# One core, one encoder block: weights of two column tiles interleaved word by word, and moving buffers shifted by 64 bytes

## The chip, the cores and the metric

The kernel runs on one NeuronCore of a Trainium2 chip. The number that counts is device time in microseconds for one execution. "Span" is the time from the first to the last instruction in a profiled execution; the time of that same execution also takes in what lies around it.

Five engines work side by side: TensorE (PE in the rows; its weight loads are listed as PEld), VectorE (DVE), ScalarE (ACT), GpSimd (POOL) and SyncE (SP), which issues the DMAs. A matrix product on TensorE has two operands in SBUF: the stationary one (up to 128 columns, brought in by a weight load) and the moving one (here up to 512 columns, streamed through).

## The reference, cut to what matters

```python
h = _rmsnorm(x, norm_g)                      # 512 tokens x 2048
proj = h @ w_in                              # 2048 x 10304: A's q, k, v, gate; B's cq, ckv, kr, gate; merge gates
oa = _diff_attention(...)                    # 8 heads, two softmaxes per head, 512 x 512
ya = (norm(oa) * silu(ag)) @ w_oa            # 1024 x 2048
q, kv = norm(cq) @ w_uq, norm(ckv) @ w_ukv   # 512-wide latents, 8 heads
ob = _mla_attention(...)
yb = (ob * silu(bg)) @ w_ob
merged = sigmoid(ga) * ya + sigmoid(gb) * yb
out = _rmsnorm(x + merged @ w_out, final_g)
```

Everything is float32.

## The kernel before

**Three products for one.** Each float32 operand is kept as two float32r parts, `hi` (a rounded copy) and `lo` (what the rounding left). The helper `three` issues for each 128 x 128 stationary tile three matmuls into the same PSUM tile: hi with hi (line 2115 of the profile), stationary hi with moving lo (line 2116) and stationary lo with moving hi (line 2117). Every matmul is preceded by its own weight load, so the high stationary tile is loaded twice in a row and then the low one once. Nearly all of the kernel's matmuls come from `three` with 512 moving columns; the attention's value products (`pv`) have 256, transposes (lines 2168, 2460, 2598) have 128.

**Stages, in order of time.** First (about 0 to 480 us) the value columns and the merge gates: `h_hi`/`h_lo` are stationary, the weights `m_hi`/`m_lo` move; five groups of 1024 columns go through a Strassen scheme whose sums of blocks are the stationary `s12_hi`, `s12_lo`, `s34_hi`, `s34_lo`. Then the eight heads of branch A, the compressed latents of B, and the eight heads of B (about 480 to 1100 us). Here `project` takes a weight piece of 1024 words per partition (eight column tiles of 128) as the stationary operand and `h_hi`/`h_lo` move; `up` does the same with `c_hi`/`c_lo` moving; `rotary_keys` uses a full tile and a half tile of 64 columns. Between the tiles of a piece lie the matmuls of the attention of the previous head (`a_extras`, `b_extras`: scores, transposes, value products). In `token_values` and in the Y stage (about 1100 to 1240 us, the products with `w_oa` and `w_ob`) the same weight buffers are the moving operand instead. Last comes the product with `w_out`, again by the Strassen scheme.

**How a weight piece gets ready.** A DMA puts it into one of four slots of `w_raw`; ScalarE copies it to `w_hi` (`split_hi`, line 781); VectorE subtracts and writes `w_lo` over `w_raw` (`split_lo`, line 1385); TensorE waits on `lo_ready`. The splits run two pieces ahead of their use (`AHEAD`).

**Addresses.** Every SBUF tensor has a fixed place, given in KB from a base that is a multiple of 2 KB. Tiles start at multiples of 512 bytes within them. So every stationary and every moving operand of the 512-column matmuls starts at the same position of a 512-byte grid.

Of the kernel before, what the change touches and what calls it, by code (L numbers as in the profile page):

```python
# [24 lines left out]
P = 128  # L25
# [17 lines left out]
AHEAD = 2  # L43
# [28 lines left out]

HALF_T, HALF_K = SEQ // 2, KT // 2
M_GROUPS, GROUP = 5, 1024
OUT_G = M_GROUPS
# [153 lines left out]
def hybrid_encoder(nc, x, positions, norm_g, w_in, lam_q1, lam_k1, lam_q2, lam_k2, a_subln_g, w_oa,  # L229
                   q_norm_g, w_uq, kv_norm_g, w_ukv, w_ob, w_out, final_g, consts, out):  # L230
    ctx = ExitStack()
    with ctx:
        KB = 1024
        base = (nc.sbuf_base + 2 * KB - 1) // (2 * KB) * (2 * KB)

        def at(name, kb, shape, dt=F32):
            return nc.alloc_sbuf_tensor_at(name, shape, dt, offset=base + int(kb * KB))
# [8 lines left out]
        spare = at("spare", 0, [P, KT, SEQ])  # L246
        h_raw1 = at("h_raw1", 144, [P, KT, HALF_T])
# [11 lines left out]
        post_x = at("post_x", 156, [P, 2 * SEQ])  # L259
        m_hi = at("m_hi", 160, [P, M_HI, 4 * SEQ], F32R)  # L260
        s34_raw = at("s34_raw", 184, [P, HALF_K, 2, HALF_T])
        s34_lo = at("s34_lo", 184, [P, HALF_K, 2, HALF_T], F32R)
        post_z = at("post_z", 200, [P, 2 * SEQ])

# [6 lines left out]
        w_hi = at("w_hi", 112, [P, SLOTS, 1024], F32R)  # L271
        c_hi = at("c_hi", 128, [P, 2 * LT, SEQ], F32R)
        rope_n = at("rope_n", 128, [P, SEQ])
        c_lo = at("c_lo", 144, [P, 2 * LT, SEQ], F32R)
# [64 lines left out]
        v_raw = at("v_raw", 202, [P, TOK, P])  # L339
        ones_sq = at("ones_sq", 204, [P, P], F32R)  # L340
        cst = at("cst", 204.5, [P, P + 2])
        small = at("small", 205.03125, [P, 160])
# [3 lines left out]
        assert base + 206 * KB - 336 <= nc.sbuf_usable_end  # L346

# [430 lines left out]
        def _(act):  # L778
            def split_hi(piece, cols=2 * HALF_PIECE):
# [418 lines left out]
            for s in range(C_STEPS):  # L1198
                if s == VB_STEP:
                    a_step(s, Head(HEADS, C0), False, True)  # L1200
                split_hi(Piece(C0 + s + AHEAD), HALF_PIECE if s == C_STEPS - 1 else 2 * HALF_PIECE)
# [86 lines left out]
            for s in range(2):  # L1288
                split_hi(Piece(B0 + B_STEPS * last + s + AHEAD))
                b_step(s, last, LAST_PAIR, True, True)  # L1290
# [10 lines left out]
            for s in range(Y_STEPS):  # L1301
                if s >= Y_STEPS - AHEAD:
                    merge_hi(OUT0 + s + AHEAD - Y_STEPS)
                elif s not in (2, 3):
                    split_hi(Piece(Y0 + s + AHEAD))
                if s < 2:
# [5 lines left out]
                if s in (2, 3):  # L1312
                    split_hi(Piece(Y0 + s + AHEAD))
                if s == 2:
# [59 lines left out]
        def _(dve):  # L1374
# [6 lines left out]

            def split_lo(piece, cols=2 * HALF_PIECE):

                dve.wait_ge(hi_ready, piece.after(0))
                dve.tensor_tensor(w_lo[:, piece.slot, 0:cols], w_raw[:, piece.slot, 0:cols],  # L1385
                                  w_hi[:, piece.slot, 0:cols].bitcast(F32), ALU.subtract).then_inc(lo_ready, 1)

# [477 lines left out]
            def kr_split_lo(piece):  # L1865
                dve.wait_ge(hi_ready, piece.after(0))
                of_tiles = w_hi[:, piece.slot, :].rearrange("p (k c) -> p k c", k=8)[:, :, B_ROPE:2 * B_ROPE]
                raw_tiles = w_raw[:, piece.slot, :].rearrange("p (k c) -> p k c", k=8)[:, :, B_ROPE:2 * B_ROPE]
                dve.tensor_tensor(of_tiles, raw_tiles, of_tiles.bitcast(F32), ALU.subtract).then_inc(lo_ready, 1)

            for s in range(C_STEPS):
                if KR_STEP <= s + AHEAD < VB_STEP:
                    kr_split_lo(Piece(C0 + s + AHEAD))
                else:
                    if s == VB_STEP:
                        a_step(s, Head(HEADS, C0), False, True)
                    split_lo(Piece(C0 + s + AHEAD), HALF_PIECE if s == C_STEPS - 1 else 2 * HALF_PIECE)
                if s < VB_STEP:
# [83 lines left out]
            for s in range(2):  # L1962
                split_lo(Piece(B0 + B_STEPS * last + s + AHEAD))
                b_step(s, last, LAST_PAIR, True, True)
# [39 lines left out]
            for s in range(Y_STEPS):  # L2004
# [3 lines left out]
                if s == Y_STEPS - 1:  # L2008
                    merge_lo(OUT0)
                elif s < Y_STEPS - AHEAD and s not in (2, 3):  # L2010
                    split_lo(Piece(Y0 + s + AHEAD))
                if s < 2:
# [5 lines left out]
                if s in (2, 3):  # L2018
                    split_lo(Piece(Y0 + s + AHEAD))
                for head in GATED_AT.get(s, ()):  # L2020
# [91 lines left out]
        def _(pe):  # L2112
# [5 lines left out]

            def tile(piece, c0, width=P):
                return w_hi[:, piece.slot, c0:c0 + width], w_lo[:, piece.slot, c0:c0 + width]  # L2120

            def project(piece, dst, half, halves, rhs_hi, rhs_lo, k0, midway=None):

                pe.wait_ge(lo_ready, piece.after(0))
                for k in range(8):
                    if k == 4 and midway:
                        midway()
                    hi, lo = tile(piece, k * P)
# [334 lines left out]
            def rotary_keys(s):  # L2463
                piece = Piece(C0 + s)
                pe.wait_ge(lo_ready, piece.after(0))
                for k in range(8):
                    if k == 4:
                        tail(2 * s)
                    kt = 8 * (s % 2) + k
                    both = w_hi[:, piece.slot, k * P:(k + 1) * P]  # L2470
                    high = w_hi[:, piece.slot, k * P:k * P + B_ROPE]
                    if kt == 0:
# [13 lines left out]
            def token_values(g):  # L2486
                pieces = [Piece(C0 + VB_STEP + 2 * g + half) for half in range(2)]
                for t in range(TOK):
# [7 lines left out]
                    for kt in range(LT):  # L2496
                        if t == 0 and kt % 2 == 0:
                            pe.wait_ge(lo_ready, pieces[kt // 2].after(0))
                        hi, lo = tile(pieces[kt // 2], kt % 2 * SEQ, SEQ)
                        last = three(SC[2 + j % 2][:, :], c_hi[:, kt, q], c_lo[:, kt, q], hi, lo, kt == 0, kt == LT - 1)  # L2500
# [18 lines left out]

            def up(piece, c0, dst, which, stride=2 * P):  # L2520
                for k in range(LT):
                    hi, lo = tile(piece, k * stride + c0)
                    last = three(dst[:, :], hi, lo, c_hi[:, which * LT + k, :], c_lo[:, which * LT + k, :],
# [21 lines left out]
            def b_up(h, pair, prev):  # L2545
# [6 lines left out]
                if pair[1] == LOW:  # L2552
                    if prev:
                        pe.wait_ge(rope_cos, pair[0])
                    up(piece, P, TR, 1).then_inc(rope_up, 1)
                pe.wait_ge(acc_read, g - 1)
                up(piece, 0, b_banks(pair)[0], 1, 2 * P if pair[1] == LOW else P).then_inc(used, 1)
# [4 lines left out]
                up(piece, 0, b_banks(pair)[1], 0, P).then_inc(used, 1)  # L2562
                b_extras(1, h, pair, True, prev)
# [18 lines left out]
            def y_block(u, i, t, halves):  # L2582
# [3 lines left out]
                for k in range(2):  # L2586
                    hi, lo = tile(Piece(Y0 + U_STEPS * u + i), k * SEQ, SEQ)
                    kt = 2 * i + k
# [102 lines left out]
```

## Time and profile before

| | |
|---|---|
| median of 3 runs | 1430.33 us (1429.76 to 1430.56) |
| time of the profiled execution | 1429.3 us |
| span of the profiled execution | 1427.5 us |
| TensorE busy | 1413.2 us (99% of the span), 6604 matmuls |
| VectorE busy | 1020.0 us |
| ScalarE busy | 707.1 us |

The profiled execution took 1.8 us more than its span, and is 1.0 us below the median. "Busy" of TensorE is modelled from pipelined matmuls that overlap each other, so the time from the start of one matmul to the start of the next (called a gap below) tells more than the duration of one.

### The profile page before, as it was taken

What the parts mean: (1) busy time and instruction counts of PE and PEld (TensorE: products, weight loads), DVE (VectorE), ACT (ScalarE), POOL (GpSimd) and SP (SyncE); (2) the same over time, 40 slices, a digit from 0 to 9 for tenths busy, and PEclk for the clock granted to TensorE, in tenths of its full rate; (3) what the DMA queues carried; (4) which work ended last, traced back from release to release, by engine and by line L of the source; (5) the groups of instructions that cost most, each with busy time, mean ns of one, the idle gap of its engine ahead of it and who ended that gap; (6) DMA issues with size and microseconds to landing.
All of it is one profiled execution on the core that took longest, in us unless ns stands there. A gap on an engine that the chain in (4) does not pass through costs nothing.

```text
span 1427.5 us, 17881 instructions
## 1 busy us (share of the span) xinstructions
PE 1413.2 (99%) x6604; PEld 1175.1 (82%) x6604; DVE 1020.0 (71%) x1381; ACT 707.1 (50%) x894; POOL 31.5 (2%) x52
## 2 busy tenths in 40 slices
PE   8999999999999999999999999999999999999997
PEld 7888888888888888888888878888888888888886
DVE  6967898798878868677667656666676353478966
ACT  6546334544344456665666667555564222324434
POOL 0000000000000000000000000000000000000000
PEclk9999999999999999999999999999999999999999
DMA  8439576766756543222222434322242444617674
GB/s 300 145 125 316 177 263 186 236 213 212 238 184 207 184 146 83 79 82 81 81 81 82 114 106 133 84 72 66 81 140 74 151 125 152 207 45 247 197 254 172
DMA packets 182976, 218.43 MB, mean 153 GB/s; under 512 B 19456, under 2 KB 133248, under 8 KB 182272
## 3 DMA queue, kind: packets, MB, share of 16 engines
q1 hardware_dynamic: 174304, 197.64, 44.5%
q10 hardware_dynamic: 8608, 19.93, 3.6%
q8 instruction: 41, 0.67, 0.2%
q14 instruction: 23, 0.19, 0.0%
HBM read 195.51 MB, written 22.02 MB: 152 GB/s over the span
## 4 chain that ended last, share of the span: by engine, by line
PE 91%; DVE 3%; DMA 1%; ACT 1%; issue 1%; SPq 1%; POOL 0%; DVEq 0%; POOLq 0%; ACTq 0%
PE duo L2115 28%; PE duo L2117 28%; PE duo L2116 28%; PE duo L2168 2%; DMA start_y<-start_columns 1%; PE duo L2142 1%; PE duo L2145 1%; SPq L610 1%; ACT m_hi L886 1%; PE duo L2159 1%; PE duo L2164 1%; PE duo L2163 1%; PE duo L2160 1%; PE duo L2161 1%; PE duo L2598 0%
## 5 line engine op out<-in xcount | busy, mean ns | idle before, releaser
L1385 DVE TENSOR_TENSOR w_lo<-w_raw,w_hi 128x1024 fp32r<-128x1024 f32 (+1 forms) x116 | 135.3, 1167 | 99.3 <-ACT w_hi L781 98.7
L2115 PE MATMUL duo<-h_hi,w_hi 128*128 128x512 f32 x512 | 201.8, 394 | 0.0
L2117 PE MATMUL duo<-h_hi,w_lo 128*128 128x512 f32 x512 | 199.6, 390 | 0.0
L2116 PE MATMUL duo<-h_lo,w_hi 128*128 128x512 f32 x512 | 199.6, 390 | 0.0
L886 ACT ACTIVATE m_hi<-m_raw 128x2048 fp32r<-128x2048 f32 (+1 forms) x66 | 115.5, 1752 | 144.6 <-PE duo L2117 71.5
L781 ACT ACTIVATE w_hi<-w_raw 128x1024 fp32r<-128x1024 f32 (+1 forms) x118 | 119.2, 1011 | 124.3 <-DMA w_raw<-in_w_ob_dram 65.8
L1502 DVE TENSOR_TENSOR m_lo<-m_raw,m_hi 128x2048 fp32r<-128x2048 f32 (+3 forms) x71 | 141.9, 2001 | 26.9 <-ACT m_hi L886 26.5
L2115 PE MATMUL duo<-m_hi,h_hi 128*128 128x512 f32 x368 | 144.6, 393 | 1.6 <-DVE h_lo L1538 0.9
L2117 PE MATMUL duo<-m_hi,h_lo 128*128 128x512 f32 x368 | 143.3, 389 | 0.0
L2115 PE MATMUL duo<-m_hi,s_hi 128*128 128x512 f32 x320 | 124.5, 389 | 0.0
L2117 PE MATMUL duo<-m_hi,s_lo 128*128 128x512 f32 x320 | 124.5, 389 | 0.0
L2116 PE MATMUL duo<-m_lo,h_hi 128*128 128x512 f32 x300 | 116.8, 389 | 0.0
L2117 PEld LDWEIGHTS duo<-h_hi,w_lo 128*128 128x128 f32 x512 | 96.1, 188 | 20.6
L2116 PEld LDWEIGHTS duo<-h_lo,w_hi 128*128 128x128 f32 x512 | 96.3, 188 | 18.7
L2115 PEld LDWEIGHTS duo<-h_hi,w_hi 128*128 128x128 f32 x512 | 96.2, 188 | 18.7
L2116 PE MATMUL duo<-m_lo,s_hi 128*128 128x512 f32 x224 | 87.1, 389 | 0.0
L2115 PEld LDWEIGHTS duo<-m_hi,h_hi 128*128 128x128 f32 x368 | 69.1, 188 | 19.3 <-DVE m_lo L1502 2.4
L2117 PEld LDWEIGHTS duo<-m_hi,h_lo 128*128 128x128 f32 x368 | 69.1, 188 | 14.5
L1396 DVE TENSOR_TENSOR pt<-duo,pt 128x512 fp32r<-128x512 f32 x64 | 42.7, 687 | 45.7 <-ACT pt L794 45.5
L801 ACT ACTIVATE e<-e,small 128x512 f32<-128x512 f32 x64 | 45.8, 716 | 50.0 <-DVE small L1416 50.0
L2117 PEld LDWEIGHTS duo<-m_hi,s_lo 128*128 128x128 f32 x320 | 60.1, 188 | 12.5
L794 ACT ACTIVATE pt<-duo 128x512 fp32r<-128x512 f32 x64 | 36.3, 595 | 68.7 <-PE duo L2168 67.0
(322 smaller groups left out, 2991.0 us busy)
## 6 DMA issues: line engine op xcount, KB each, us to landing
m_raw<-in_w_in_dram SPq DMA_DIRECT2D x110, 512.0 KB, 4.7
w_raw<-in_w_in_dram SPq DMA_DIRECT2D x132, 256.0 KB, 3.0
o_raw<-in_w_out_dram SPq DMA_DIRECT2D x32, 512.0 KB, 5.1
spare<-in_w_in_dram SPq DMA_DIRECT2D x17, 512.0 KB, 4.6
h_raw<-in_w_in_dram SPq DMA_DIRECT2D x17, 512.0 KB, 4.9
w_raw<-in_w_oa_dram SPq DMA_DIRECT2D x32, 256.0 KB, 3.3
sig<-gates SPq DMA_DIRECT2D x8, 1024.0 KB, 6.3
w_raw<-in_w_ob_dram SPq DMA_DIRECT2D x32, 256.0 KB, 3.4
```

What stands on the lines that cost most here:

```text
L610: sp.dma_start(dst, src).then_inc(m_in[st.raw], 16)
L781: act.activation(w_hi[:, piece.slot, 0:cols], w_raw[:, piece.slot, 0:cols], ACT.Copy).then_inc(hi_ready, 1)
L794: act.activation(pt[:, 0, :, (t % 2) * P:(t % 2 + 1) * P], src[:, :].rearrange("p (k c) -> p k c", k=TOK), ACT.Copy).then_inc(pt_hi_ready, 1)
L801: last = act.activation(e[:, t % 2, m, :], e[:, t % 2, m, :], ACT.Exp, bias=nm[:, b:b + 1], scale=A_SCALE, accum_out=sums[:, b:b + 1])
L886: act.activation(hi_of(st, 0, st.parts), raw_of(st, 0, st.parts), ACT.Copy).then_inc(m_hi_ready, 1)
L1385: dve.tensor_tensor(w_lo[:, piece.slot, 0:cols], w_raw[:, piece.slot, 0:cols], w_hi[:, piece.slot, 0:cols].bitcast(F32), ALU.subtract).the ...
L1396: dve.tensor_tensor(pt[:, 1, :, c], src[:, :].rearrange("p (k c) -> p k c", k=TOK), pt[:, 0, :, c].bitcast(F32), ALU.subtract).then_inc(pt ...
L1502: dve.tensor_tensor(lo_of(st, p0, p1), raw_of(st, p0, p1), hi_of(st, p0, p1).bitcast(F32), ALU.subtract).then_inc(done, 1)
L2115: pe.matmul(dst, lhs_hi, rhs_hi, start=start, stop=False)
L2116: pe.matmul(dst, lhs_hi, rhs_lo, start=False, stop=False)
L2117: return pe.matmul(dst, lhs_lo, rhs_hi, start=False, stop=stop)
L2168: last = pe.transpose(dst[:, k * P:(k + 1) * P], src[:, k * P:(k + 1) * P], ident)
```

## The change

It has two parts.

First, the layout of `w_hi` when it is used as the stationary operand. Before, its column tiles lay one after the other. Now the first half and the second half of a piece alternate word by word: word 0 of tile 0, word 0 of tile 4, word 1 of tile 0, and so on. ScalarE's copy reads `w_raw` in order and writes with a step of two words; VectorE's subtraction reads `w_hi` with a step of two; the weight load of a high tile reads 128 words with a step of two (a tile covers 1024 bytes instead of 512). `w_lo` stays as it was, since it lies over `w_raw`. Pieces that are used as the moving operand (`moving=True`) keep the old layout. `kr_split_lo` follows the new layout with one more dimension.

Second, the places. The base becomes a multiple of 512 bytes. At 32, 144 and 184 KB 512 bytes are left free, and `h_hi`, `m_hi`, `c_hi`, `s34_lo` and some more (`spare`, `s34_raw`, `post_z`, `rope_n`, `ones_sq`, `cst`, `small`) start 64 bytes past the grid. `h_lo`, `m_lo`, `c_lo`, `w_hi`, `w_lo`, `s12_hi`, `s12_lo`, `s34_hi` and the operands of attention and of the last stages stay on it.

```diff
+BANKS, ROOM_AT, MOVED_BY = 512, (32, 144, 184), 64
+def in_halves(columns):
+    return columns.rearrange("p (j q) -> p j q", j=2)
+def in_pairs(columns):
+    return columns.rearrange("p (q j) -> p j q", j=2)
...
-        base = (nc.sbuf_base + 2 * KB - 1) // (2 * KB) * (2 * KB)
+        base = (nc.sbuf_base + BANKS - 1) // BANKS * BANKS
+        def at(name, kb, shape, dt=F32, off=0):
+            room = BANKS * sum(kb >= edge for edge in ROOM_AT)
+            return nc.alloc_sbuf_tensor_at(name, shape, dt, offset=base + int(kb * KB) + room + off)
...
-        h_hi = at("h_hi", 0, [P, KT, SEQ], F32R)
+        h_hi = at("h_hi", 0, [P, KT, SEQ], F32R, off=MOVED_BY)
-        m_hi = at("m_hi", 160, [P, M_HI, 4 * SEQ], F32R)
+        m_hi = at("m_hi", 160, [P, M_HI, 4 * SEQ], F32R, off=MOVED_BY)
-        s34_lo = at("s34_lo", 184, [P, HALF_K, 2, HALF_T], F32R)
+        s34_lo = at("s34_lo", 184, [P, HALF_K, 2, HALF_T], F32R, off=MOVED_BY)
-        c_hi = at("c_hi", 128, [P, 2 * LT, SEQ], F32R)
+        c_hi = at("c_hi", 128, [P, 2 * LT, SEQ], F32R, off=MOVED_BY)
...
-                act.activation(w_hi[:, piece.slot, 0:cols], w_raw[:, piece.slot, 0:cols], ACT.Copy
-                               ).then_inc(hi_ready, 1)
+                dst, src = w_hi[:, piece.slot, 0:cols], w_raw[:, piece.slot, 0:cols]
+                if not moving:
+                    dst, src = in_pairs(dst), in_halves(src)
+                act.activation(dst, src, ACT.Copy).then_inc(hi_ready, 1)
...
+                dst, src, hi = (a[:, piece.slot, 0:cols] for a in (w_lo, w_raw, w_hi))
+                if not moving:
+                    dst, src, hi = in_halves(dst), in_halves(src), in_pairs(hi)
+                dve.tensor_tensor(dst, src, hi.bitcast(F32), ALU.subtract).then_inc(lo_ready, 1)
...
-            def tile(piece, c0, width=P):
-                return w_hi[:, piece.slot, c0:c0 + width], w_lo[:, piece.slot, c0:c0 + width]
+            def high_tile(piece, k, tiles=8):
+                half = tiles // 2
+                c0 = k % half * P
+                return in_pairs(w_hi[:, piece.slot, 0:tiles * P])[:, k // half, c0:c0 + P]
+            def tile(piece, k, tiles=8):
+                return high_tile(piece, k, tiles), w_lo[:, piece.slot, k * P:(k + 1) * P]
```

## Rows read from the trace of the kernel before

**Rows 1.** The page: engines' busy time, and the slices of TensorE and its clock.

```profile
PE 1413.2 (99%) x6604; PEld 1175.1 (82%) x6604; DVE 1020.0 (71%) x1381; ACT 707.1 (50%) x894; POOL 31.5 (2%) x52
PE   8999999999999999999999999999999999999997
PEclk9999999999999999999999999999999999999999
```

**Rows 2.** The page: the chain that ended last, shares by engine.

```profile
PE 91%; DVE 3%; DMA 1%; ACT 1%; issue 1%; SPq 1%; POOL 0%; DVEq 0%; POOLq 0%; ACTq 0%
```

**Rows 3.** Waits of TensorE: us in total, times, longest (six rows in all).

```profile
PE duo L2216 <- DMA cst<-in_consts_dram: 2.6, 1, 2.6
...
PE duo L2115 <- DVE h_lo L1502: 0.3, 1, 0.3
```

**Rows 4.** Groups of TensorE's matmuls, shapes apart: busy us, mean ns of one (tiles: moving, stationary).

```profile
L2115 PE MATMUL duo<-h_hi,w_hi 128*128 128x512 f32 x512 | 201.8, 394 | 0.0
...
L2116 PE MATMUL duo<-h_lo,w_hi 128*128 128x512 f32 x512 | 199.6, 390 | 0.0
...
L2115 PE MATMUL duo<-m_hi,s_hi 128*128 128x512 f32 x320 | 124.5, 389 | 0.0
...
L2115 PE MATMUL duo<-c_hi,w_hi 128*128 128x512 f32 x80 | 32.5, 406 | 0.0
...
L2474 PE MATMUL duo<-h_lo,w_hi 128*64 128x512 f32 x16 | 6.4, 410 | 0.0
L2476 PE MATMUL duo<-h_hi,w_hi 128*128 128x512 f32 x15 | 5.9, 393 | 0.0
```

**Rows 5.** TensorE's timeline in the Y stage, first and last of 178 rows: start us, us.

```profile
1104.78 0.39 PE L2115 MATMUL duo<-w_hi,ga_hi 128*128 128x512 f32 x1
...
1144.90 0.39 PE L2115 MATMUL duo<-w_hi,gb_hl 128*128 128x512 f32 x1
```

**Rows 6.** TensorE's timeline in an A head: a value product and the projection behind it.

```profile
552.56 0.28 PE L2115 MATMUL duo<-pt,v_hl 128*128 128x256 f32 x1
552.67 0.28 PE L2116 MATMUL duo<-pt,v_hl 128*128 128x256 f32 x1
...
553.87 0.28 PE L2117 MATMUL duo<-pt,v_hl 128*128 128x256 f32 x1
553.99 0.40 PE L2115 MATMUL duo<-h_hi,w_hi 128*128 128x512 f32 x1
554.23 0.40 PE L2116 MATMUL duo<-h_lo,w_hi 128*128 128x512 f32 x1
554.46 0.39 PE L2117 MATMUL duo<-h_hi,w_lo 128*128 128x512 f32 x1
...
555.15 0.39 PE L2117 MATMUL duo<-h_hi,w_lo 128*128 128x512 f32 x1
```

**Rows 7.** The chain in order of time, one group of four transposes in an A head.

```profile
591.33 0.44 PE duo L2168 x4
```

**Rows 8.** Groups of weight loads, shapes apart: busy us, mean ns of one.

```profile
L2116 PEld LDWEIGHTS duo<-h_lo,w_hi 128*128 128x128 f32 x512 | 96.3, 188 | 18.7
...
L2474 PEld LDWEIGHTS duo<-h_lo,w_hi 128*64 128x64 f32 x16 | 2.1, 134 | 0.6
```

**Rows 9.** Timeline of the weight loads in an A head.

```profile
609.89 0.19 PEld L2116 LDWEIGHTS duo<-h_lo,w_hi 128*128 128x128 f32 x1
```

**Rows 10.** TensorE's timeline from the same moment, first and last of 12 rows.

```profile
609.89 0.39 PE L2115 MATMUL duo<-h_hi,w_hi 128*128 128x512 f32 x1
...
612.38 0.39 PE L2117 MATMUL duo<-h_hi,w_lo 128*128 128x512 f32 x1
```

**Rows 11.** Line 781, the copy to `w_hi`: duration ns min/median/max.

```profile
L781 ACT ACTIVATE w_hi<-w_raw x118: 615/1053/1067, 481.0 to 1237.6; 128x1024 fp32r<-128x1024 f32 x106, 128x512 fp32r<-128x512 f32 x12
```

**Rows 12.** Line 1385, the subtraction to `w_lo`, and who waited for it (no row follows).

```profile
L1385 DVE TENSOR_TENSOR w_lo<-w_raw,w_hi x116: 680/1224/1230, 484.6 to 1238.7; 128x1024 fp32r<-128x1024 f32 x104, 128x512 fp32r<-128x512 f32 x12
...
who waited for it (us, times):
```

**Rows 13.** Busy time by stretch: PE, PEld, DVE, ACT, POOL, clock, DMA share, GB/s.

```profile
600.00:650.00 50.00, 50.00 (x240) 41.62 (x239) 34.44 (x70) 32.21 (x52) 4.28 (x6) 1.00 0.28 80
```

More of the change, by code:

```diff
@@ L1200, in _ @@
                     a_step(s, Head(HEADS, C0), False, True)
-                split_hi(Piece(C0 + s + AHEAD), HALF_PIECE if s == C_STEPS - 1 else 2 * HALF_PIECE)
+                split_hi(Piece(C0 + s + AHEAD), HALF_PIECE if s == C_STEPS - 1 else 2 * HALF_PIECE,
+                         moving=VB_STEP <= s + AHEAD < C_STEPS)
                 if s < VB_STEP:
@@ L1288, in _ @@
             for s in range(2):
-                split_hi(Piece(B0 + B_STEPS * last + s + AHEAD))
+                split_hi(Piece(B0 + B_STEPS * last + s + AHEAD), moving=True)
                 b_step(s, last, LAST_PAIR, True, True)
@@ L1304, in _ @@
                 elif s not in (2, 3):
-                    split_hi(Piece(Y0 + s + AHEAD))
+                    split_hi(Piece(Y0 + s + AHEAD), moving=True)
                 if s < 2:
@@ L1312, in _ @@
                 if s in (2, 3):
-                    split_hi(Piece(Y0 + s + AHEAD))
+                    split_hi(Piece(Y0 + s + AHEAD), moving=True)
                 if s == 2:
@@ L1876, in _ @@
                         a_step(s, Head(HEADS, C0), False, True)
-                    split_lo(Piece(C0 + s + AHEAD), HALF_PIECE if s == C_STEPS - 1 else 2 * HALF_PIECE)
+                    split_lo(Piece(C0 + s + AHEAD), HALF_PIECE if s == C_STEPS - 1 else 2 * HALF_PIECE,
+                             moving=VB_STEP <= s + AHEAD < C_STEPS)
                 if s < VB_STEP:
@@ L1962, in _ @@
             for s in range(2):
-                split_lo(Piece(B0 + B_STEPS * last + s + AHEAD))
+                split_lo(Piece(B0 + B_STEPS * last + s + AHEAD), moving=True)
                 b_step(s, last, LAST_PAIR, True, True)
@@ L2010, in _ @@
                 elif s < Y_STEPS - AHEAD and s not in (2, 3):
-                    split_lo(Piece(Y0 + s + AHEAD))
+                    split_lo(Piece(Y0 + s + AHEAD), moving=True)
                 if s < 2:
@@ L2018, in _ @@
                 if s in (2, 3):
-                    split_lo(Piece(Y0 + s + AHEAD))
+                    split_lo(Piece(Y0 + s + AHEAD), moving=True)
                 for head in GATED_AT.get(s, ()):
@@ L2117, in three, with columns @@
                 return pe.matmul(dst, lhs_lo, rhs_hi, start=False, stop=stop)
-            def tile(piece, c0, width=P):
-                return w_hi[:, piece.slot, c0:c0 + width], w_lo[:, piece.slot, c0:c0 + width]
+            def columns(piece, c0):
+                return w_hi[:, piece.slot, c0:c0 + SEQ], w_lo[:, piece.slot, c0:c0 + SEQ]
+            def high_tile(piece, k, tiles=8):
[4 more added lines that the diff above has]
+                return high_tile(piece, k, tiles), w_lo[:, piece.slot, k * P:(k + 1) * P]
             def project(piece, dst, half, halves, rhs_hi, rhs_lo, k0, midway=None):
@@ L2127, in project @@
                         midway()
-                    hi, lo = tile(piece, k * P)
+                    hi, lo = tile(piece, k)
                     last = three(dst[:, :], hi, lo, rhs_hi[:, k0 + k, :], rhs_lo[:, k0 + k, :],
@@ L2469, in rotary_keys @@
                     kt = 8 * (s % 2) + k
-                    both = w_hi[:, piece.slot, k * P:(k + 1) * P]
-                    high = w_hi[:, piece.slot, k * P:k * P + B_ROPE]
+                    both = high_tile(piece, k)
+                    high = both[:, 0:B_ROPE]
                     if kt == 0:
@@ L2498, in token_values @@
                             pe.wait_ge(lo_ready, pieces[kt // 2].after(0))
-                        hi, lo = tile(pieces[kt // 2], kt % 2 * SEQ, SEQ)
+                        hi, lo = columns(pieces[kt // 2], kt % 2 * SEQ)
                         last = three(SC[2 + j % 2][:, :], c_hi[:, kt, q], c_lo[:, kt, q], hi, lo, kt == 0, kt == LT - 1)
@@ L2518, in _, with up @@
                 token_values(g)
-            def up(piece, c0, dst, which, stride=2 * P):
+            def up(piece, j, dst, which, each=2):
                 for k in range(LT):
-                    hi, lo = tile(piece, k * stride + c0)
+                    hi, lo = tile(piece, k * each + j, LT * each)
                     last = three(dst[:, :], hi, lo, c_hi[:, which * LT + k, :], c_lo[:, which * LT + k, :],
@@ L2554, in b_up @@
                         pe.wait_ge(rope_cos, pair[0])
-                    up(piece, P, TR, 1).then_inc(rope_up, 1)
+                    up(piece, 1, TR, 1).then_inc(rope_up, 1)
                 pe.wait_ge(acc_read, g - 1)
-                up(piece, 0, b_banks(pair)[0], 1, 2 * P if pair[1] == LOW else P).then_inc(used, 1)
+                up(piece, 0, b_banks(pair)[0], 1, 2 if pair[1] == LOW else 1).then_inc(used, 1)
                 b_extras(0, h, pair, True, prev)
@@ L2561, in b_up @@
                 pe.wait_ge(acc_read, g)
-                up(piece, 0, b_banks(pair)[1], 0, P).then_inc(used, 1)
+                up(piece, 0, b_banks(pair)[1], 0, 1).then_inc(used, 1)
                 b_extras(1, h, pair, True, prev)
@@ L2586, in y_block @@
                 for k in range(2):
-                    hi, lo = tile(Piece(Y0 + U_STEPS * u + i), k * SEQ, SEQ)
+                    hi, lo = columns(Piece(Y0 + U_STEPS * u + i), k * SEQ)
                     kt = 2 * i + k
```

28 lines of the change are left out of this document (12 added, 16 removed).

## The prediction

> **What bounds the kernel now.** I read the page first: TensorE is busy 99% of the span and its clock is granted in full (2.4 GHz) in every slice [rows 1]. The chain that ended last is TensorE for 91% [rows 2]. Then its waits: six single waits from 2.6 us down to 0.3 us, none for a weight piece [rows 3]. So neither data nor another engine sets the time; the end is the sum of the gaps from one matmul's start to the next. Whatever does not shorten or lengthen a gap costs nothing.
>
> Then how long a gap is. In a long undisturbed stretch 177 gaps take 1144.90 - 1104.78 = 40.12 us, which is 226.7 ns or 544 cycles of 2.4 GHz for 512 columns [rows 5]. In an A head, with `h` moving and weights stationary, 11 gaps take 2.49 us, 226 ns [rows 10]. The 256-column products have 10 gaps in 553.87 - 552.67 = 1.20 us, 120 ns or 288 cycles [rows 6]. Both are the column count plus 32 cycles (13.3 ns). That surplus is what the change can act on: 13.3 ns of 226.7, or 6%.
>
> **Is the surplus a fixed price?** Three readings say no. The gap moves with circumstances: the first gap of the value product is 0.11 us, not 0.12, and after it the first projection gaps are 0.24 and 0.23 us; the five gaps from 553.99 to 555.15 take 1.16 us, 232 ns each [rows 6], before they settle to 226 [rows 10]. Nothing but the phase between stream and weight load differs there. Second, the four transposes take 0.44 us, 110 ns each, in the chain; that is two cycles a column (106.7 ns) and 3 ns over; so they pay only 3 ns beside their columns, though each loads 128 columns of weights too [rows 7]. Third, the two reads run at different paces: a load of 128 columns takes 188 ns, one of 64 takes 134 ns, so a column costs 54 / 64 = 0.84 ns, two cycles [rows 8], while the stream takes one column a cycle. Load and matmul start together (609.89 both) [rows 9, 10], at the same position of the 512-byte grid. With a step of one word the stream covers twice the bytes per cycle that the load does, so within one load (256 cycles) it gains 512 bytes on it and passes it once, modulo the grid. In the transposes both go at the same pace and never pass. My reading is that passing costs the 32 cycles.
>
> With a step of two words the load covers 8 bytes in two cycles, the pace of the stream, and 64 bytes of offset hold the two apart. By this reading the surplus goes in exactly the gaps in which a moved buffer (`h_hi`, `c_hi`) streams while a high tile with a step of two is loaded.
>
> **How many gaps.** In a triple, the gap from line 2115 to 2116 has `h_hi` or `c_hi` moving and the second load of the high tile beneath it: 512 + 80 = 592 [rows 4]. The gap from 2116 to 2117 streams the unmoved low part and loads the unchanged `w_lo`: no change. The gap from 2117 to the next triple has the moved high part again, and loads a high tile if a triple follows directly. If all did, that would be 592 more, and 31 for the rotary keys [rows 4], 1215 in all; followed in order of time on TensorE it is 1092, since the rest are followed by attention's matmuls.
>
> **What one is worth.** The transposes leave 3.3 ns over their columns [rows 7], so the gap can come down to 213.3 + 3 = about 216 ns, a saving of 10.9 ns: 1092 x 10.9 = 11.9 us. The bounds are 0 and the whole 13.3 ns, 14.5 us. I take 10.9, the nearest row's remainder. The disturbed gaps behind attention's matmuls (232 instead of 226) might give some tenths more; I count none.
>
> The Trainium skill ("TensorE: Matmul & The Clock Gate", section "Back-to-back issue gap") gives N/2.4 + 2.5 ns for a warm gap, 215.8 ns here; the trace has 226.7. By that page's number as the floor the sum would be the same to 0.1 us. The same page ("Step-by-step: what each phase is for") says that stream and weight load have independent read ports and that loading does not steal bandwidth from the matmul; by that rule the change would do nothing, and it is rival two below.
>
> **What else the edit touches.** (a) Strided loads under unmoved streams: a high tile now also follows `ka_lo`, `pt`, `h_lo` of the rotary keys, `vT_lo` and `kr_lo`, 82 times in order of time. There both run at the same pace from the same position. If they blocked each other all the way, a gap could grow by the load's 256 cycles, 106.7 ns, 8.7 us in all; the transposes, which are just that case, pay 3 ns [rows 7], so I take 0. (b) Unstrided loads whose position against the stream changes by 64 bytes: `m_hi` over `s12_hi`/`s34_hi` in 2 x 320 gaps [rows 4], and some 220 more (`m_lo` over `s34_lo`, weights over `c_hi`). The stream still passes the load once. The nearest rows are the gaps at other phases: 0.11 us where 0.12 is settled, 0.24 where 0.227 is [rows 6], so -10 to +13 ns, -8.6 to +11.2 us over 860 gaps. Since disturbed gaps return to 226 by themselves, I take 0. (c) ScalarE's strided copy and VectorE's strided read. No strided one-word access is in the trace. Lower bound nothing; upper bound, each takes twice as long: 1.05 and 1.22 us more a piece [rows 11, 12]. Nobody waited for `w_lo` [rows 12], it is made two pieces ahead, and with about seven pieces in 50 us VectorE would rise from 34.4 to some 43 us and ScalarE from 32.2 to 40 us of 50 [rows 13]. Cost 0 under TensorE's stream; if the cover went, the first loss would be at attention's transposes, which wait for softmax on VectorE. (d) The new base and the free 512 bytes: no instruction changes, 0.
>
> **Sum.** 1429.3 us of the profiled execution, minus 11.9, is 1417.4; the median lay 1.0 us above that execution, so 1418.4. I say 1418.
>
> **Rivals.**
> 1. Only part of the surplus goes (the offset clears one of the two gap kinds, or the gap ends between 224 and 218 ns, or (a) and (b) take some back): 1092 gaps at 2.7 to 8 ns, 3 to 9 us, time 1421 to 1427.5. For it: the settled 226.7 is the result of something that locks itself after every disturbance [rows 6], and such things seldom vanish whole; 500 of the gaps lie behind an unchanged slow gap.
> 2. The surplus is fixed for float32r and the change does nothing: 1430. For it: +32 cycles at both 256 and 512 columns. Against: the phase dependence and the transposes.
> 3. Slower. Each stretch of weights read takes its cycles from the stream: 128 contiguous words cost 32 cycles, one for four words; with a step of two the same words lie in twice as many such stretches and cost 64. That adds 13.3 ns to each of the 1215 or so strided loads: 16.2 us, 1446.5. For it: 32 is the same at 256 and 512 columns, as a price of the load must be, and the transposes, streaming at half pace, would have the room to absorb it. Against: the gaps of 0.24 and 0.11, which a fixed theft would not give. It decides as soon as a strided load costs more than it saves, by 2.4 ns (2.9 us over 1215, 0.2% of the time). The Trainium skill ("SBUF — State Buffer", section "Door 1: The DMA port swizzle") says that accesses keep full bandwidth with at least two hits per 16-byte line, which a step of two float32 words just has; by it this rival would not occur, but no row here shows it.
>
> **Numbers.** Forecast (1414 to 1421) 0.48; rival 1 (1421 to 1427.5) 0.20; rival 2 (within 2.9 us, 0.2%, of 1430.3, about what a measurement can tell from no change) 0.12; rival 3 or another loss 0.17; more than 16 us gained 0.03. So faster 0.71, same 0.12, slower 0.17. The range 1412.5 to 1431.5 leaves out rival 3 and the far gain.
>
> **What would show it.** Right: in A and B heads, starts of triples 216, 227, 216 ns apart, so a triple takes about 658 instead of 680 ns, while the Strassen and Y stages keep 226.7; more matmuls per 50 us between 480 and 1100 us, none elsewhere; the end some 12 us earlier. Wrong: 226.7 after line 2115 (rival 2), 240 there (rival 3), changed gaps with `m_hi` moving (b), waits of TensorE for `w_lo` or for softmax (c).

## The result, and the profile after

The changed kernel takes 1446.55 us (median of 4 runs, 1445.75 to 1447.21), the kernel before 1430.43 us beside it: ratio 1.0115, 95% interval 1.0102 to 1.0128. It is 16.1 us slower, where 12 us less was forecast. The profiled execution took 1446.0 us, its span is 1444.2 us, 16.7 us more than before.

The page, engines' busy time, and TensorE's slices of busy time and clock:

```profile
PE 1429.5 (99%) x6604; PEld 1183.0 (82%) x6604; DVE 1020.5 (71%) x1381; ACT 713.3 (49%) x894; POOL 31.5 (2%) x52
...
PE   8999999999999999999999999999999999999997
...
PEclk9999999999999999999999999999999999999999
```

The same number of matmuls at the same clock keep TensorE busy for 16.3 us more. VectorE gained 0.5 us and ScalarE 6.2 us of work [rows 1], both beside TensorE. Its waits (largest, and smallest of the seven rows) are of the size of before [rows 3], and none is for a weight piece:

```profile
PE duo L2240 <- DMA cst<-in_consts_dram: 2.8, 1, 2.8
...
PE duo L2131 <- DVE mg_lo L1517: 0.2, 1, 0.2
```

So the gaps grew. Groups of matmuls and of weight loads with shapes apart (line 2131 is the former 2115):

```profile
L2131 PE MATMUL duo<-h_hi,w_hi 128*128 128x512 f32 x512 | 204.1, 399 | 0.0
...
L2132 PE MATMUL duo<-h_lo,w_hi 128*128 128x512 f32 x512 | 201.3, 393 | 0.0
...
L2131 PE MATMUL duo<-m_hi,s_hi 128*128 128x512 f32 x320 | 126.2, 395 | 0.0
```

```profile
L2132 PEld LDWEIGHTS duo<-h_lo,w_hi 128*128 128x128 f32 x512 | 99.5, 194 | 17.8
```

The mean duration of a 512-column matmul follows the gap: a settled 389 ns stands for a gap of 226.7, so 393 to 399 are gaps of 231 to 236. The strided weight load takes 194 ns, 6 more than before [rows 8]. What the forecast did not have is the third row: `m_hi` over the block sums, with no strided load at all, went from 389 [rows 4] to 395. In an A head, TensorE's timeline at the place of [rows 10]:

```profile
609.78 0.39 PE L2131 MATMUL duo<-h_hi,w_hi 128*128 128x512 f32 x1
610.01 0.39 PE L2132 MATMUL duo<-h_lo,w_hi 128*128 128x512 f32 x1
610.24 0.39 PE L2133 MATMUL duo<-h_hi,w_lo 128*128 128x512 f32 x1
610.47 0.40 PE L2131 MATMUL duo<-h_hi,w_hi 128*128 128x512 f32 x1
610.71 0.39 PE L2132 MATMUL duo<-h_lo,w_hi 128*128 128x512 f32 x1
...
611.86 0.62 PE L2166 MATMUL duo<-ka,qa 128*128 128x512 f32 x2
```

Nine gaps take 611.86 - 609.78 = 2.08 us, 231 ns each, and no pattern of 216, 227, 216 shows: all gaps read 0.23 or 0.24 us.

**Where in time.** The view of one source line gives duration min/median/max and first and last start of each group. Of before (not shown above), then of after:

```profile
L2115 PE MATMUL duo<-h_hi,w_hi x512: 389/389/481, 491.0 to 1052.6; 128*128 128x512 f32 x171
...
L2115 PE MATMUL duo<-w_hi,ga_hi x128: 389/389/476, 1065.6 to 1232.0; 128*128 128x512 f32 x128
...
L2115 PE MATMUL duo<-o_hi,mg_hi x176: 389/389/500, 1254.4 to 1419.0; 128*128 128x512 f32 x176
```

```profile
L2131 PE MATMUL duo<-h_hi,w_hi x512: 392/394/486, 499.5 to 1068.9; 128*128 128x512 f32 x171
...
L2131 PE MATMUL duo<-w_hi,ga_hi x128: 389/389/476, 1082.1 to 1248.4; 128*128 128x512 f32 x128
...
L2131 PE MATMUL duo<-o_hi,mg_hi x176: 389/389/499, 1270.8 to 1435.7; 128*128 128x512 f32 x176
```

The first starts cut the span into four stages; the same was read for three of the experiments below.

| us, profiled executions | first stage, up to the first projection tile | heads of A and B | Y stage | last stage |
|---|---|---|---|---|
| before | 491.0 | 574.6 | 188.8 | 173.1 |
| changed | 499.5 | 582.6 | 188.7 | 173.4 |
| shift only (e2) | 499.7 | 584.6 | 188.8 | 174.1 |
| interleaving only (e3) | 490.9 | 583.5 | 188.8 | 174.0 |
| changed, `m_hi` and `s34_lo` back (e7) | 498.2 | 582.5 | 188.8 | 173.1 |

Half of the loss (8.5 us) is in the first stage, which has no strided load; the other half (8.0 us) in the heads. The Y stage and the last one, whose operands all lie on the grid and are contiguous, stayed within 0.3 us. Each row of the table is one execution: in e4 and e6 below, which take the time of the kernel before, the heads read 575.1 and 575.6 us, so a difference of 1 us between two rows says nothing.

### The profile page after: what moved, and what is told of

It is laid out like the page before. It is cut to its first block, busy times and chain, and to the rows that moved or that the text cites. A ratio compares the mean times of both kernels' runs of the same rounds, so it can differ in the third digit from the quotient of the medians.

```text
span 1444.2 us, 17881 instructions
## 1 busy us (share of the span) xinstructions
PE 1429.5 (99%) x6604; PEld 1183.0 (82%) x6604; DVE 1020.5 (71%) x1381; ACT 713.3 (49%) x894; POOL 31.5 (2%) x52
## 4 chain that ended last, share of the span: by engine, by line
PE 91%; DVE 4%; DMA 2%; ACT 1%; SPq 1%; issue 1%; POOL 0%; DVEq 0%; POOLq 0%; ACTq 0%
PE duo L2131 28%; PE duo L2133 28%; PE duo L2132 28%; PE duo L2192 2%; DMA start_y<-start_columns 1%; PE duo L2166 1%; PE duo L2169 1%; SPq L620 1%; ACT m_hi L898 1%; PE duo L2183 1%; PE duo L2184 1%; PE duo L2188 1%; PE duo L2185 1%; PE duo L2187 1%; PE duo L2622 0%
## 5 line engine op out<-in xcount | busy, mean ns | idle before, releaser
L794 ACT ACTIVATE w_hi<-w_raw 128x1024 fp32r<-128x1024 f32 (+1 forms) x118 | 125.5, 1065 | 125.3 <-DMA w_raw<-in_w_ob_dram 66.3
L2131 PEld LDWEIGHTS duo<-h_hi,w_hi 128*128 128x128 f32 x512 | 99.5, 194 | 20.3
L2132 PEld LDWEIGHTS duo<-h_lo,w_hi 128*128 128x128 f32 x512 | 99.5, 194 | 17.8
L2131 PEld LDWEIGHTS duo<-m_hi,s_hi 128*128 128x128 f32 x320 | 60.1, 188 | 13.7
```

The costliest lines, as they stand in the source:

```text
L794: act.activation(dst, src, ACT.Copy).then_inc(hi_ready, 1)
L2131: pe.matmul(dst, lhs_hi, rhs_hi, start=start, stop=False)
L2132: pe.matmul(dst, lhs_hi, rhs_lo, start=False, stop=False)
```

## The experiments

Four theories were put to the test. A: the settled gap needs consecutive streams to start at one position, and a shift between them breaks it. B: a load with a step of two takes its cycles from the stream (rival 3). C: the forecast's, a step of two and a steady shift never collide. D, formed after e1: the gap is shortest when a load starts at the same place as its stream modulo 256 bytes and is contiguous, and longer otherwise. (Modulo 256 bytes: only what is left over after whole steps of 256 bytes counts.)

**e2, the shift alone, and e3, the interleaving alone.** Both are the changed kernel with one half undone:

```diff
 # e2
 def in_pairs(columns):
-    return columns.rearrange("p (q j) -> p j q", j=2)
+    return columns.rearrange("p (j q) -> p j q", j=2)
...
-                of_tiles = w_hi[:, piece.slot, :].rearrange("p (k c j) -> p j k c", k=4, j=2)[:, :, :, B_ROPE:2 * B_ROPE]
+                of_tiles = w_hi[:, piece.slot, :].rearrange("p (j k c) -> p j k c", k=4, j=2)[:, :, :, B_ROPE:2 * B_ROPE]
 # e3
-BANKS, ROOM_AT, MOVED_BY = 512, (32, 144, 184), 64
+BANKS, ROOM_AT, MOVED_BY = 512, (32, 144, 184), 0
```

> The changed kernel with the old, contiguous layout of the high weight tiles; the 64-byte shifts stay. Theory A (the shift is the whole loss): 1445 to 1448 us. Theory B (the strided loads cost, and the shift costs only where the first and last stages slowed, some 7 us): 1437 to 1438.

Measured: 1449.19 us against 1430.09, ratio 1.0137 (1.0120 to 1.0154).

> The changed kernel with the shift set to 0 bytes; the interleaved layout and the strided loads stay. Theory A: 1430 to 1431 us, no change. Theory B: 1439 to 1440, the 9 us that the heads of both branches lost, and the first stage back at 226.7 ns a gap.

Measured: 1438.69 us, ratio 1.0060 (1.0043 to 1.0077).

Neither theory stands as written. The shift alone costs 19.1 us, more than the whole change; the interleaving alone costs 8.6; together they cost 16.1, less than the sum of 27.7. The first stage loses only with the shift (8.7 and 8.5 us); the heads lose 10.0 with the shift, 8.9 with the interleaving, 8.0 with both, all well beyond 1 us, though the three are not clearly apart from each other. The group of `m_hi` over the block sums says the same, first in e2, then in e3:

```profile
L2131 PE MATMUL duo<-m_hi,s_hi 128*128 128x512 f32 x320 | 126.2, 394 | 0.0
```

```profile
L2131 PE MATMUL duo<-m_hi,s_hi 128*128 128x512 f32 x320 | 124.5, 389 | 0.0
```

**e4, everything moved together.** The kernel before with another base:

```diff
-        base = (nc.sbuf_base + 2 * KB - 1) // (2 * KB) * (2 * KB)
+        base = (nc.sbuf_base + 511) // 512 * 512 + 64
```

> The kernel before with its base 64 bytes past the grid, so that every tensor moves by the same amount. Theory A (only differences between the operands' positions count): 1430 us. If absolute positions count (64 bytes past a 512-byte line as such): 1440 or more.

Measured: 1430.05 us against 1430.09, ratio 0.9999 (0.9989 to 1.0008). Moving every operand by 64 bytes costs nothing, moving some of them (e2) costs 19.1 us: the differences between operands count. No other common shift was tried.

**e1, the matmuls by themselves.** No encoder; TensorE runs blocks of 72 matmuls on float32r parts of `x`, each block after four transposes:

```python
order = [k for _ in range(3) for k in range(8)]
turns()
for k in order: h, l, a, b = tiles(k, 64, 0, 0, 0, 2); pe.matmul(acc[:, :], h, a, **on); pe.matmul(acc[:, :], h, b, **off); pe.matmul(acc[:, :], l, a, **end)
```

> The matmuls alone, none of the encoder: 24 blocks, each four transposes and then 24 triples (high tile with high moving, high tile with low moving, low tile with high moving; 512 columns), one source line a block, so that a block's busy time less 0.16 us over 72 is its mean gap. Blocks differ in where the moving and the stationary operands start past a 512-byte grid and in the step of the high tile. Theory A (the settled gap of 226.7 ns needs consecutive streams to start at the same position; a shift between them breaks it, whatever the layout of the weights): the base block 227, everything moved by 64 together 227, both moving parts moved and the stationary ones not 227 or another settled value, only the high moving part moved 231 to 233, with or without the step of two; step of two with nothing moved 227. Theory B (a load with a step of two takes its cycles from the stream): 236 for every block with the step of two, 227 for those with only a shift. Theory C (the record's: a step of two and a steady shift of 64 never collide): 216 to 220 in the block with both moving parts moved and a step of two.

TensorE's timeline in settled parts, the 24th and the 72nd matmul of a block, 48 gaps apart: the base (line 76); both moving parts at 64 bytes with a step of two (line 84); everything at 64 bytes (line 94); both moving parts at 256 (line 102).

```profile
47.27 0.39 PE L76 MATMUL acc<-move_hi,still_lo 128*128 128x512 f32 x1
...
58.15 0.40 PE L76 MATMUL acc<-move_hi,still_lo 128*128 128x512 f32 x1
...
115.83 0.40 PE L84 MATMUL acc<-move_hi,still_lo 128*128 128x512 f32 x1
...
127.03 0.40 PE L84 MATMUL acc<-move_hi,still_lo 128*128 128x512 f32 x1
...
201.43 0.39 PE L94 MATMUL acc<-move_hi,still_lo 128*128 128x512 f32 x1
...
212.31 0.40 PE L94 MATMUL acc<-move_hi,still_lo 128*128 128x512 f32 x1
...
269.90 0.39 PE L102 MATMUL acc<-move_hi,still_lo 128*128 128x512 f32 x1
...
280.78 0.39 PE L102 MATMUL acc<-move_hi,still_lo 128*128 128x512 f32 x1
```

10.88 us over 48 gaps is 226.7 ns; 11.20 us is 233.3. Each block ran in one execution alone, but the base block stands two or three times in each of e1, e5, e8 and e10 and settles at 226.7 ns all nine times. All blocks, mean of the last 24 gaps, worked out in the same way from the timeline (high moving / low moving / high stationary / low stationary, bytes past the grid):

| contiguous | ns | step of two for the high tile | ns |
|---|---|---|---|
| 0/0/0/0, 64/64/64/64, 256/256/0/0, 256/0/0/0 | 226.7 | 0/0/0/0 | 233.3 |
| 64/64/0/0 | 228.9 | 64/64/0/0 | 233.3 |
| 64/0/0/0 | 233.3 | 64/0/0/0 (the change) | 232.2 |
| 64/0/64/0 (first stage of the change) | 233.3 | 256/256/0/0 | 231.1 |
| 0/0/64/64 | 233.3 | 32/32/0/0, 448/448/0/0 | 233.3 |
| 0/0/0/64 | 231.1 | 128/128/0/0 | 232.2 |
| 32/32, 96/96, 448/448 (over 0/0) | 233.3 | step of four, 0/0/0/0 | 233.3 |
| 128/128, 384/384 (over 0/0) | 232.7 | | |
| 448/0/0/0 | 234.4 | | |

Theory C (the forecast's) is wrong: the block made for it takes 233.3. Theory B is wrong in size: 233.3, not 236, and a step of four costs no more than one of two. Theory A is half right: the shift breaks the settled gap, but so does moving both streams alike (228.9), and shifting by 256 does not. What remains of theory D is this: every contiguous block at 226.7 has all four operands at the same place modulo 256 bytes, and every other block is 2 to 9 ns longer. Which two operands have to match, the table does not say. In 64/0/64/0 each load starts at the same place as the stream that it runs under (a load starts together with the matmul before its own [rows 9, 10]), and still the gap is 233.3. And 64/0/0/0, where only the high stream is off, is worse than 64/64/0/0, where both are (233.3 against 228.9). So the distance from a load to a stream is not all that counts; the shift between consecutive streams, which theory A names, may be the rest, but no block isolates it.

The blocks carry over to the whole kernel. In the heads, the 1776 gaps of `project` and `up`, without those that hold a wait (300 ns or more), have a mean of 227.8 ns before, 232.9 with the shift alone, 233.0 with the interleaving alone and 231.9 with both; the blocks say 226.7, 233.3, 233.3 and 232.2.

**e6, e7, e9, the distance in the whole kernel.** e6 is e2 with `MOVED_BY` 256; e9 is the changed kernel with 256; e7 the changed kernel with

```diff
-        m_hi = at("m_hi", 160, [P, M_HI, 4 * SEQ], F32R, off=MOVED_BY)
-        s34_raw = at("s34_raw", 184, [P, HALF_K, 2, HALF_T], off=MOVED_BY)
-        s34_lo = at("s34_lo", 184, [P, HALF_K, 2, HALF_T], F32R, off=MOVED_BY)
+        m_hi = at("m_hi", 160, [P, M_HI, 4 * SEQ], F32R)
+        s34_raw = at("s34_raw", 184, [P, HALF_K, 2, HALF_T])
+        s34_lo = at("s34_lo", 184, [P, HALF_K, 2, HALF_T], F32R)
```

> The shift-only kernel (contiguous weights, the same buffers moved) with 256 instead of 64 bytes. Theory D (the distance between stream and load counts modulo 256 bytes): 1430 to 1431 us, the whole loss of the 64-byte shift gone. If any shift between consecutive streams breaks the settled gap: 1445 or more, as with 64 bytes.

Measured: 1430.13 us against 1430.32, ratio 1.0000 (0.9991 to 1.0010). The same edit that costs 19.1 us at 64 bytes costs nothing at 256.

> The changed kernel with the moved buffers 256 instead of 64 bytes past the grid, interleaving kept. Theory D: the first stage is back at 226.7 ns, the heads keep what the step of two costs: 1436 to 1439 us, like the kernel with the interleaving alone (1438.7). If the two edits of the change need each other (a step of two pays only with a shift): 1430 or below.

Measured: 1438.69 us against 1430.14, ratio 1.0059 (1.0043 to 1.0076), as e3. A step of two pays at neither distance.

> The changed kernel with `m_hi`, `s34_raw` and `s34_lo` back on the grid; `h_hi`, `c_hi` and the interleaving stay. Theory D: the products with the block sums get 226.7 ns back (320 triples, 960 gaps at some 5 ns, 4.8 us), those with `h_hi` stationary do not, since it still lies 64 bytes off its stream: 1441 to 1442 us. If a moved buffer costs only while it streams: all 687 triples of the first stage are free again, some 9 us, 1437 to 1438.

Measured: 1444.99 us against 1430.32, ratio 1.0104 (1.0087 to 1.0120), 1.6 us less than the changed kernel, not 4.8. The groups with `h_hi` and with the block sums stationary:

```profile
L2131 PE MATMUL duo<-m_hi,h_hi 128*128 128x512 f32 x368 | 146.8, 399 | 1.2 <-DVE h_lo L1553 0.8 <-DVE m_lo L1517 0.2 <-DVE h_lo L1517 0.2
...
L2131 PE MATMUL duo<-m_hi,s_hi 128*128 128x512 f32 x320 | 125.4, 392 | 0.0
```

The block sums came from 395 to 392, not back to 389, though stream and load lay at one place again, and `h_hi` went from 398 to 399. Summed from the traces, the 960 gaps with block sums stationary take 219.0 us before, 222.4 in the changed kernel and 220.3 here; the 1070 gaps with `h_hi` or `h_lo` stationary take 244.4, 249.9 and 250.5. So only 3.4 us were there to win back, not 4.8; 2.1 came back, and 0.6 more were lost beside them. e10 asks why not all 3.4.

**e5, the forecast's mechanism in its purest form, and the size of a load.**

> Blocks of 24 triples again, one source line each, now with all stationary tiles of a block in the same layout. (a) Every load with a step of two, moving parts 0, 32, 64, 96, 128, 192, 256, 320, 384 and 448 bytes past the grid. The record's theory in its purest form (stream and load at one pace, held apart): 216 to 220 ns at some of these distances. Theory D (the 32 cycles are the least that a load costs its stream, and any distance that is not a multiple of 256 bytes, or a step of two, adds up to 16 more): 229 to 235 at all, never under 226.7. (b) Contiguous tiles of 96, 64 and 32 columns at distance 0: if the surplus is paid per word loaded, 24, 16 and 8 cycles over 512 instead of 32, so 223, 220 and 217 ns; if it is fixed, 226.7. (c) Contiguous, 448, 384 and 256 moving columns: 200, 173 and 120 ns if the surplus stays 32 cycles.

The block at 64 bytes with a step of two on every stationary tile, and the best distance found, 448 bytes:

```profile
98.95 0.39 PE L84 MATMUL acc<-move_hi,still_lo 128*128 128x512 f32 x1
...
110.15 0.40 PE L84 MATMUL acc<-move_hi,still_lo 128*128 128x512 f32 x1
...
219.10 0.39 PE L98 MATMUL acc<-move_hi,still_lo 128*128 128x512 f32 x1
...
230.15 0.39 PE L98 MATMUL acc<-move_hi,still_lo 128*128 128x512 f32 x1
```

That is 233.3 and 230 ns (192 bytes gives the same). With all loads strided, the settled gaps at 0, 32, 64, 96, 128, 192, 256, 320, 384 and 448 bytes are 235.6, 233.3, 233.3, 233.3, 231.4, 230.0, 233.3, 233.3, 231.6, 230.0: never under 226.7. Contiguous at 192 and 320 bytes gives 233.3 and 228.9, the values of 448 and 64, so the contiguous pattern repeats after 256 bytes (0 and 256, 64 and 320, 128 and 384, 192 and 448 agree). With a step of two 0 and 256 bytes do not agree, 235.6 and 233.3. (b) failed its expectation: tiles of 96, 64 and 32 columns take 230.0, 230.0 and 231.7, more than a full tile. The surplus is not a price per word loaded. (c) 448, 384 and 256 moving columns take 202.8, 173.3 and 120.0: 39, 32 and 32 cycles over the columns. With 256 moving columns at distance 0 a step of two on every load costs nothing: 120.0 as well. So a strided load has no fixed price; with 512 moving columns it costs 6.6 ns and more.

**e8, other forms.**

> Blocks of 24 triples again, contiguous unless said. It asks what the 32 cycles belong to. If they come from the weight load meeting the stream: with bfloat16 operands (half the bytes on both sides) the surplus is another one, and changes with the position of the stream as the float32r one does; with 64 rows instead of 128 nothing changes, 226.7. If they are fixed for a matmul of 512 columns with a weight load, whatever is read: 226.7 for bfloat16 too, at 0, 32, 64 and 128 bytes. Streams with a step of two words and loads with a step of one, two or four: theory D says each is at least 226.7, and most 229 to 236. Contiguous at 160 and 224 bytes: 229 to 234.

The bfloat16 block, 48 gaps in 10.36 us:

```profile
231.26 0.38 PE L101 MATMUL acc<-half_move_hi,half_still_lo 128*128 128x512 bf16 x1
...
241.62 0.38 PE L101 MATMUL acc<-half_move_hi,half_still_lo 128*128 128x512 bf16 x1
```

215.8 ns, six cycles over 512, at 0, 32, 64 and 128 bytes and with a step of two on the loads alike, and from the first gap behind the transposes on. So the other 26 cycles, and the dependence on position as far as it was tried, come with float32r. With 64 rows it stays 226.7. A stream with a step of two takes 451 to 456 ns, whatever its loads do. A step of four on all loads: 235.0. Contiguous at 160 and 224 bytes: 234.3 and 233.3.

**e10, settling.** Runs of n aligned triples in turn with runs of n triples as in the change, and float32r in turn with bfloat16:

```python
for j in range(0, 48, 16):  # runs of 8
    for k in range(8): [pe.matmul(...) for ... in three(k, 0, 1)]
    for k in range(8): [pe.matmul(...) for ... in three(k, 64, 2)]
```

> Matmuls alone again. Part one: runs of n triples with stream and load at distance 0 and contiguous, in turn with runs of n triples as in the change (64 bytes, step of two on every stationary tile), n = 1, 2, 4, 8. It asks why putting `m_hi` back on the grid gave 1.6 us where 4.8 were expected. If a stream needs some six to twelve gaps at distance 0 to settle, the aligned runs of 1 and 2 triples stay at 230 to 234 ns and only runs of 8 come near 228. If each gap depends only on its own two operands: 227 in the aligned runs at every n. Part two: a float32r and a bfloat16 product in turn, each with its own weight load, with the float32r operands at distance 0 or 64 bytes, contiguous or with a step of two. The load of a product runs under the product before it. If the surplus of 26 cycles over bfloat16 belongs to loading float32r weights, the gap behind the bfloat16 stream is the long one (226 ns or more) and the one behind the float32r stream is 216; if it belongs to streaming float32r, the other way round; if it takes both, a pair of gaps takes 432 ns, whatever the distance. If distance matters in the pairs too, the 64-byte blocks are longer than the others.

TensorE's timeline at the start of an aligned run of eight triples (line 110), behind a shifted one:

```profile
187.14 0.40 PE L110 MATMUL acc<-move_hi,still_hi 128*128 128x512 f32 x1
187.37 0.39 PE L110 MATMUL acc<-move_lo,still_hi 128*128 128x512 f32 x1
187.60 0.39 PE L110 MATMUL acc<-move_hi,still_lo 128*128 128x512 f32 x1
187.83 0.40 PE L110 MATMUL acc<-move_hi,still_hi 128*128 128x512 f32 x1
...
188.99 0.39 PE L110 MATMUL acc<-move_hi,still_lo 128*128 128x512 f32 x1
...
192.39 0.39 PE L110 MATMUL acc<-move_hi,still_lo 128*128 128x512 f32 x1
```

The first eight gaps take 1.85 us, 231 ns each; the next 15 take 3.40 us, 227. The aligned runs average 232.3, 229.5, 229.7 and 227.9 ns at n = 1, 2, 4 and 8, the shifted ones between them 229.9, 231.9, 233.0 and 233.2. So a gap depends on more than its own two operands, and an aligned run is at 226.7 only from about its eighth gap on. But the mean of both kinds together is 230.6 to 231.4 ns at every n: what short aligned runs lack, the short shifted runs beside them have gained, and the length of the runs hardly matters for the sum.

This accounts for what e7 won back. There the block sums and `h_hi` take turns after twelve matmuls, at times after twenty-four:

```profile
251.55 0.39 PE L2131 MATMUL duo<-m_hi,s_hi 128*128 128x512 f32 x1
...
254.28 0.40 PE L2131 MATMUL duo<-m_hi,h_hi 128*128 128x512 f32 x1
...
257.08 0.39 PE L2131 MATMUL duo<-m_hi,s_hi 128*128 128x512 f32 x1
```

The twelve over the block sums take 2.73 us, 227.5 ns each, the next twelve 2.80 us, 233.3. The 960 gaps over the block sums average 229.5 ns, and runs of n = 4, which are twelve matmuls too, 229.7.

The second part tells less than it should. A float32r and a bfloat16 product in turn take 458 ns (contiguous, 0 bytes), 464 (64 bytes), 461 and 458 (step of two, 0 and 64 bytes), more than the 226.7 + 215.8 = 442.5 of each kind among its own. The trace splits a pair into 0.42 us from the float32r matmul's start to the bfloat16 one's and 0.04 us from there to the next, which fits none of the three expectations. Changing the type costs time itself, so whether the 26 cycles come with loading float32r, with streaming it or with both stays open.

## Why the prediction was wrong

**The step that failed** is "Is the surplus a fixed price?", with its conclusion "passing costs the 32 cycles" and a step of two at 64 bytes frees the gap. Of its three readings, the first was right in what it concluded: gaps do depend on where the operands lie against each other. But every departure from the settled 226.7 that the trace showed over a few gaps together went upward (232 over five gaps behind the value product [rows 6]). The single low gap, 0.11 us, was taken as proof that a gap can be shorter; it was a transient of the 256-column products. Of the 5679 gaps between two 512-column matmuls in the trace of before, none is under 224 ns, and in the 53 blocks of e1, e5 and e8 with 512 float32r columns moving no settled mean is under 226.7. The kernel before sat at the best position that any block found; a change of position could at most keep it. The second reading compared unlike things: transposes of float32 were taken as float32r at half pace. The measured half-pace float32r stream (e8) takes 451 ns or more, 59 cycles over its 1024, not 3 ns. The third reading (a load takes two cycles a column, a stream one) did not carry the conclusion: with a step of two and any of ten distances the gap is 230 to 236. The gaps in the heads that were to fall by 10.9 ns rose: without the waits, from 227.8 to 232.6 ns behind line 2115 and from 227.9 to 232.1 behind 2117. The gap behind 2116, set down as "no change", went from 227.6 to 231.0.

The size had a slip of its own: the "nearest row's remainder" of 3.3 ns leaves 13.3 - 3.3 = 10.0 ns to save, not 10.9, so 10.9 us and not 11.9. It matters little beside a step with the wrong sign.

**The price of (b), 0,** was the other miss. Unstrided loads whose distance to the stream changed cost the first stage 8.5 us, within the stated -8.6 to +11.2. The argument "disturbed gaps return to 226 by themselves" holds only when the operands lie at one place; a lasting shift lasts. It also counted too few gaps: `m_hi` over `h_hi`, both moved alike, slowed too (its group's mean went from 393 to 398 ns). `m_lo` and `h_lo` between them were not moved, and e1 has 233.3 for that arrangement (64/0/64/0) where moving all four gives 226.7.

**(a)** The gaps with a strided load under `ka_lo` (32) went from 226.7 to 229.9 ns, those under `vT_lo` and `kr_lo` (14) rose by some 4 ns, those under `pt` (20) fell from 120.0 to 118.2. That is 0.1 us in all; 0 was near enough.

**(c)** was right. The copy with a step of two and the subtraction, by line:

```profile
L794 ACT ACTIVATE w_hi<-w_raw x118: 651/1121/1164, 488.8 to 1254.9; 128x1024 fp32r<-128x1024 f32 x106, 128x512 fp32r<-128x512 f32 x12
```

```profile
L1401 DVE TENSOR_TENSOR w_lo<-w_raw,w_hi x116: 679/1224/1227, 492.5 to 1256.0; 128x1024 fp32r<-128x1024 f32 x104, 128x512 fp32r<-128x512 f32 x12
...
who waited for it (us, times):
```

ScalarE's median went from 1053 to 1121 ns, VectorE's stayed 1224 [rows 11, 12], and still nobody waits. **(d)** was right: e6 has the new base and the free 512 bytes and takes the time of before.

**Rival 3** gives 1446.5 and the chip gave 1446.55. That is chance. It charged 13.3 ns to each of 1215 strided loads and nothing elsewhere. In fact the interleaving alone costs 8.6 us (6.6 ns a gap in e1), and also in gaps without a strided load (`h_lo` streaming over the load of `w_lo`: 227.6 ns on average in the timeline of before, 232.6 in e3's); a step of four costs no more than a step of two in e1, where twice the stretches should have doubled the price; at 256 moving columns a step of two costs nothing (e5); and half of the loss lies where no load is strided. That it would not occur at all, as its last sentence has it, is not borne out either: at 512 float32r columns a step of two does cost something (226.7 to 233.3 ns). **Rival 2** was wrong for float32r; its band also ran to 1433.2 us, a little beyond the stated range. The independent read ports of the Trainium skill ("TensorE: Matmul & The Clock Gate", "Step-by-step: what each phase is for") fit e8 for bfloat16, 215.8 ns at every position tried, which is also what N/2.4 + 2.5 gives there. For float32r the runs differ from both, 226.7 at best and up to 7.7 ns more by position alone.

What stays open is the cause beneath. Dependence on distance with a period of 256 bytes looks like two readers meeting in one part of the memory, but no run saw such a meeting. None says which pair of operands has to match, or what the 26 cycles at distance 0 are.

## What to carry to other kernels

Before trading on a deviation from a steady gap, ask whether the steady one is a ceiling or a floor: read which way every lasting departure goes, and measure the steady gap alone in a block of some seventy matmuls per arrangement, of which two dozen fit into one run. For float32r, start every stationary and every moving operand at the same place modulo 256 bytes and keep stationary tiles contiguous; moving all of them together is free, moving some is not. Do not price single gaps of a mixed arrangement from uniform blocks: for about eight matmuls behind a change a gap still depends on what went before. In e10, aligning half of the triples was worth 1.9 to 2.7 ns a gap on average, whatever the length of the runs; aligning all is worth 6.6.

## What the runs showed of the hardware that was not expected

- A float32r matmul of 512 columns with its load settles at 226.7 ns (32 cycles over 512) at the best, a bfloat16 one at 215.8 (six over).
- The float32r gap depends on where moving and stationary operands start against each other, with a period of 256 bytes for contiguous ones: with both moving parts off both stationary ones by the same distance, 226.7 at 0, 228.9 at 64, 232.7 at 128, 233.3 at 192. bfloat16 took 215.8 at each of the four positions tried.
- Narrower stationary tiles (96, 64, 32 columns) take longer, 230 to 231.7 ns.
- A moving operand with a step of two float32r words halves the pace, 451 ns; a high stationary tile with a step of two costs 6.6 ns a gap (226.7 to 233.3) at 512 moving columns and distance 0, and nothing at 256 columns (120.0).
- After a disturbance, aligned float32r gaps take three to ten gaps to settle, about eight behind a shifted run.
- A float32r and a bfloat16 product in turn take 458 to 464 ns, 15 to 22 more than apart.
